# Weighing one condition vector of the second layer's modulation on GpSimd instead of TensorE

## The reference, cut to what matters

```
c_act = jax.nn.silu(c)
for layer in range(DEPTH):
    mod = c_act @ w_ada[layer] + b_ada[layer]
    sh1, sc1, g1, sh2, sc2, g2 = jnp.split(mod[:, None, :], 6, axis=-1)
    h = rmsnorm(x, mix_norm_g[layer]) * (1.0 + sc1) + sh1
    y = ...                      # layer 1: differential attention with 8 heads
    x = x + g1 * y
    h = rmsnorm(x, ffn_norm_g[layer]) * (1.0 + sc2) + sh2
    x = x + g2 * hierarchical_moe(h, ...)
```

```
bias = jnp.where(allowed[None], -slopes[:, None, None] * dist[None], -jnp.inf)
s1 = einsum(qa, k1) * scale + bias;   s2 = einsum(qb, k2) * scale + bias
p = softmax(s1) - lam * softmax(s2);  o = p @ v
```

## Time and profile before

| what | value |
|---|---|
| median of 3 runs | 1230.32 us (1229.67 to 1231.67) |
| the profiled execution: its own time | 1232.17 us |
| the profiled execution: its span | 1230.3 us |
| PE busy | 893.5 us (73%) |
| DVE busy | 350.8 us (29%) |
| ACT busy | 169.9 us (14%) |
| POOL busy | 23.6 us (2%), 70 instructions |
| DMA | 490.05 MB, mean 398 GB/s |
| chain that ended last | DMA 50%, PE 41%, SP's queue 3%, DVE 3% |

### The profile page before, as it was taken

The page is one execution under the profiler, slowest core; times in us unless marked ns, Lnnn a source line. Parts: engine busy times, 40 slices in busy tenths (PEclk is TensorE's granted clock), DMA queues, the critical chain, the costliest instruction groups (busy, mean ns, idle before and its releaser), DMA issues.

```text
span 1230.3 us, 14582 instructions
## 1 busy us (share of the span) xinstructions
PE 893.5 (73%) x6026; PEld 436.7 (35%) x6026; DVE 350.8 (29%) x893; ACT 169.9 (14%) x408; POOL 23.6 (2%) x70
## 2 busy tenths in 40 slices
PE   6999997747474756656799999966475665665647
PEld 5867453222131312121278554632131212121212
DVE  2298544121111111111124647521111111202111
ACT  1124340000000000000133353300000000000000
POOL 1001100000000000000000100000000000000000
PEclk9999999788787878787899999988787878777888
DMA  9999999999999999999995959699999999999996
GB/s 344 395 400 409 412 398 421 428 428 426 428 428 429 427 429 428 430 426 428 400 408 212 346 218 362 256 425 425 428 429 427 427 429 429 428 429 427 428 425 263
DMA packets 63224, 490.05 MB, mean 398 GB/s; under 512 B 5664, under 2 KB 8113, under 8 KB 39616
## 3 DMA queue, kind: packets, MB, share of 16 engines
q1 hardware_dynamic: 60656, 486.56, 95.4%
q10 hardware_dynamic: 2512, 2.69, 0.6%
HBM read 488.18 MB, written 1.05 MB: 398 GB/s over the span
## 4 chain that ended last, share of the span: by engine, by line
DMA 50%; PE 41%; SPq 3%; DVE 3%; issue 1%; ACT 1%; POOL 0%; DVEq 0%; ACTq 0%
PE psum L1649 41%; DMA weight_ring<-in_moe_w_down 18%; DMA weight_ring<-in_moe_w_gate 17%; DMA weight_ring<-in_moe_w_up 14%; SPq L499 2%; DMA weight_ring<-in_w_ada 1%; SPq L522 1%; DVE h_or_mix_T L1126 0%; PE psum L1748 0%; DVE ada_partials L1567 0%; ACT phase_region L907 0%; ACT phase_region L1027 0%; DVE phase_region L1601 0%; DVE phase_region L1213 0%; DVE phase_region L1096 0%
## 5 line engine op out<-in xcount | busy, mean ns | idle before, releaser
L1649 PE MATMUL psum<-weight_ring,h_or_mix_T 128*32 128x512 f32 (+1 forms) x2240 | 384.3, 711 | 232.3 <-DMA weight_ring<-in_moe_w_gate 140.8
L1649 PEld LDWEIGHTS psum<-weight_ring,h_or_mix_T 128*32 128x32 f32 (+1 forms) x2240 | 119.0, 136 | 479.1 <-issue 477.2
L1649 PE MATMUL psum<-weight_ring,ada_partials 128*32 128x512 f32 (+1 forms) x1088 | 141.2, 675 | 77.7 <-DMA weight_ring<-in_moe_w_down 72.8
L1649 PE MATMUL psum<-phase_region 128*128 128x128 f32 (+5 forms) x824 | 154.8, 349 | 4.1 <-DVE x_tokens L1377 1.3
L1649 PEld LDWEIGHTS psum<-phase_region 128*128 128x128 f32 (+2 forms) x824 | 99.4, 188 | 75.7 <-issue 54.8
L1649 PE MATMUL psum<-h_or_mix_T,weight_ring 128*128 128x256 f32 (+1 forms) x528 | 115.0, 374 | 2.8 <-DVE h_or_mix_T L1126 2.7
L1649 PEld LDWEIGHTS psum<-h_or_mix_T,weight_ring 128*128 128x128 f32 x528 | 97.3, 190 | 17.4 <-DVE h_or_mix_T L1126 1.9
L1649 PEld LDWEIGHTS psum<-weight_ring,ada_partials 128*32 128x32 f32 x1088 | 41.0, 126 | 168.2 <-issue 158.7
L1426 DVE SCALAR_TENSOR_TENSOR phase_region<-phase_region,psum 128x512 f32<-128x512 f32 x16 | 11.0, 688 | 235.6 <-ACT phase_region L940 235.6
L1442 DVE TENSOR_TENSOR phase_region<-psum,gate_rows 128x512 f32<-128x512 f32 x28 | 19.4, 692 | 205.5 <-PE psum L1649 205.5
L1431 DVE SCALAR_TENSOR_TENSOR ada_partials<-phase_region,psum 128x512 f32<-128x512 f32 x16 | 16.8, 1051 | 211.9 <-PE psum L1649 211.9
(11 more groups left out here) (222 smaller groups left out, 486.7 us busy)
## 6 DMA issues: line engine op xcount, KB each, us to landing
weight_ring<-in_moe_w_up SPq DMA_DIRECT2D x64, 2048.0 KB, 20.2
weight_ring<-in_moe_w_gate SPq DMA_DIRECT2D x62, 2048.0 KB, 20.3
weight_ring<-in_moe_w_down SPq DMA_DIRECT2D x60, 2048.0 KB, 19.7
weight_ring<-in_w_ada SPq DMA_DIRECT2D x10, 3072.0 KB, 21.3
weight_ring<-in_odd_w_in SPq DMA_DIRECT2D x6, 2048.0 KB, 22.9
weight_ring<-in_w_ada SPq DMA_DIRECT2D x10, 1024.0 KB, 23.2
weight_ring<-in_w_ada SPq DMA_DIRECT2D x4, 2048.0 KB, 17.7
weight_ring<-in_even_w_in SPq DMA_DIRECT2D x3, 2048.0 KB, 21.0
```

Source lines behind the costliest of these rows:

```text
L1649: return pe.matmul(out_, lhsT, rhs, start=first, stop=last, **kw)
```

## The change

Row 10 is no longer summed by 32 matmuls. GpSimd multiplies each of the eight rows of the slab, in its slot, by the condition's column and adds rows 1 to 7 onto row 0: 8 multiplications and 7 additions of 128x1024, each linked to the next by a semaphore. They are written in pairs of rows in front of the bias tiles of heads 2 to 5. TensorE then sums the one row that is left over the partitions with 4 matmuls, in head 4 (`add_pool_rows`) and not in head 3. `take_modulation(10)` moves from head 3 to head 4 on DVE, and the copy `CREP1` goes.

```diff
-        CREP1 = NEGS[:, :, :].rearrange("p a (k n) -> p (a k) n", n=32)
...
+        pool_weighted = sem("pool_weighted")
...
+            def weigh(n, lo, hi):
+
+                s = slab_index("ada", n)
+                rows = wide(s)
+                for k in range(lo, hi):
+                    if k == 0:
+                        pool.wait_ge(slab_in[SPOT[s]], landed(s, 0))
+                    if k == ADA_FIRST:
+                        pool.wait_ge(rest_in[SPOT[s]], landed(s, 1))
+                    link(g.tensor_scalar(rows[:, k, :], rows[:, k, :], CCOL[:, 1, k:k + 1], None, ALU.mult))
+                    if k:
+                        ins = g.tensor_tensor(rows[:, 0, :], rows[:, 0, :], rows[:, k, :], ALU.add)
+                        if k == KD - 1:
+                            ins.then_inc(pool_weighted, 1)
+                        else:
+                            link(ins)
...
             for h in range(NH):
+                if 2 <= h < 6:
+                    weigh(10, 2 * (h - 2), 2 * (h - 1))
                 if h == 0:
                     pool.wait_ge(qk_out, 16)
...
-            v.tensor_copy(CREP1[:, :, :], CCOL[:, 1, :].unsqueeze(2).broadcast_to([P, KD, 32])).then_inc(cond_in_place, 1)
...
-                if h == 3:
+                if h == 4:
                     take_modulation(10)
...
+            def add_pool_rows():
+
+                pe.wait_ge(ada_ready, 10)
+                pe.wait_ge(v_out, 4)
+                pe.wait_ge(pool_weighted, 1)
+                rows = wide(slab_index("ada", 10))[:, 0, :]
+                for g in range(4):
+                    ins = mm(PS[32 * g:32 * g + 32, ADA_BANK[10], 0:256], ONES[:, 0:32], rows[:, 256 * g:256 * g + 256],
+                             True, True, skip_group_check=True)
+                ins.then_inc(ada_summed, 1)
...
-                if h == 3:
-                    pe.wait_ge(v_out, 4)
-                    modulation_sums(10)
+                if h == 4:
+                    add_pool_rows()
```

More of the change, by code:

```diff
@@ L335, in build_trunk @@
         PART_SLOT = {6: 2, 7: 3, 5: 1}
-        ADA_HEAD = ADA_ORDER[:8]
         def sums_by(n):
@@ L1668, in modulation_sums @@
                     slab_ready(s)
-                    if n == 10:
-                        pe.wait_ge(cond_in_place, 2)
                     if n in (3, 5):
@@ L1673, in modulation_sums @@
                     elif n > 1:
-                        pe.wait_ge(ada_ready, {2: 1, 6: 2, 7: 3, 4: 4, 10: 10}[n])
-                cond = CREP if n in ADA_HEAD else CREP1
+                        pe.wait_ge(ada_ready, {2: 1, 6: 2, 7: 3, 4: 4}[n])
                 for k in range(lo, hi):
@@ L1679, in modulation_sums @@
                     for g in range(4):
-                        ins = mm(PS[32 * g:32 * g + 32, ADA_BANK[n], 0:256], cond[:, k, :], wide(s)[:, k, 256 * g:256 * g + 256],
+                        ins = mm(PS[32 * g:32 * g + 32, ADA_BANK[n], 0:256], CREP[:, k, :], wide(s)[:, k, 256 * g:256 * g + 256],
                                  k == 0, k == KD - 1, skip_group_check=True)
```

## The result

The changed kernel takes 1244.42 us (median of 4 runs, 1242.6 to 1245.23) against 1229.99 us before in the same comparison: ratio 1.0113, 95% interval 1.0101 to 1.0125, so 14.4 us slower. I had forecast 1235.4 us and a range up to 1240.0. The direction was right, the size not.

The account below looks back on a forecast made before the run. TensorE's work in the heads (700 to 757 us) was taken to move the kernel's end one for one; -3.6 + 1.4 - 0.2 + 7.5 = +5.1 us on the median 1230.3 gave 1235.4 us, range 1227.8 to 1240.0.

Parts of the forecast that it names:

- Head 3, head 4, the copy: 32 matmuls leave head 3, -3.6 us; four matmuls and `take_modulation(10)` enter head 4, +1.4; `CREP1` goes, -0.2.
- the price of the multiplication: On GpSimd, one multiplication of 1024 takes 1.04 us, drawn from fills and a bias tile; eight of them in the work.
- DVE's waits: In heads 0 to 2 DVE waits for GpSimd's instructions under way: +7.5 us, bounds 0 and 11.8.
- So no bias tile is late: GpSimd's work ends about 725 us, before `biased(5)` wants its bias tile at 727.55: no late tile.
- rival C: GpSimd itself too slow: at 3.0 us an addition, head 5's bias tile is 5.3 us late, 1233.2 us; chance 0.08.
- my own signs of being wrong: Wrong if DVE's lines keep their durations, bias tiles come late, or the last mixture starts late for want of weights.
- My upper bound: For DVE's waits: 4.4 us for each of three heads less twice 0.7, 11.8 us, if an addition takes 2.6.
- The clock is not in play: In the heads, 700 to 757 us, TensorE's clock is granted at 1.00, the 2.4 GHz level; no term for it.
- Lock or sharing: DVE and GpSimd lock each other out for a whole instruction, as the sum assumes, or share bandwidth, near the fourth case.
- rival D: DVE waits once a head for 0.8 us, no GpSimd instruction gets between its own: -1.4, 1228.9 us; chance 0.17.
- The slot: Slot 2 is free some 11 us later, in head 4; weights behind it still in time: counted 0, up to 6 us.

Follow-up runs that it names:

- none: The changed kernel with GpSimd's 15 operations on the slab left out, so row 10 is a bare row of weights: 1227.55 us.
- imm: The changed kernel with the condition's column in GpSimd's multiplications replaced by two constants, 0.5 and 0.0: 1240.61 us.
- actbias: The changed kernel, all of it computed, with the bias tiles of heads 2 to 7 made by ACT and not by GpSimd: 1237.51 us.
- prodonly: The changed kernel without GpSimd's eight multiplications and with its seven additions turned into products of two slab rows: 1238.64 us.
- multonly: The changed kernel with GpSimd's seven additions left out and its eight multiplications by the column kept: 1230.04 us.
- memset: The changed kernel with GpSimd's multiplications and additions replaced by fills of nearly the same total time: 1244.88 us.
- dve: The kernel before, with row 10 weighed by DVE in its idle time behind heads 0 to 4 and four matmuls in head 4: 1227.64 us.

## Why the prediction was right or wrong

**Head 3, head 4, the copy: right.** -3.6, +1.4 and -0.2 were forecast, -2.4 in sum; **none** measured -2.3, with both heads' periods to 0.01 us. The copy shows in the traces by itself: from the same DVE step ahead of the norm (611.99 us before, 611.85 now) to TensorE's first matmul behind it (622.63, 622.29) it is 10.64 us before and 10.44 now.

Two steps failed: the price of the multiplication and the size of DVE's waits. GpSimd's work cost 16.9 us and not 7.5; of the 9.4 us between them 3.8 go with the first and 5.6 with the second, which has a lower clock of TensorE in it.

**The price of a multiplication: wrong, and the step that failed first.** "a multiplication of 1024 is 0.51 + 640 x 0.83 = 1.04 us" took its slope from fills and its base from a bias tile, which multiplies by a constant. With a constant it is right to 0.01 us (**imm**: 1.047). The change's multiplication takes its factor from a column in SBUF, and that form had no row in the trace: 3.0 us. I gave bounds for the addition, which also had no row, and none for this. Eight times 2 us are 16 us more of GpSimd's work. From **imm** to the changed kernel it is 3.8 us of time.

**"So no bias tile is late": wrong, by that step.** With 11.6 us a head the tiles of heads 3, 4 and 5 came late and GpSimd became the pace; against **actbias** this cost 6.9 us. It is rival C, whose mechanism I priced by a dear addition and not by the multiplication, and for which I left 0.08. Late bias tiles were also one of my own signs of being wrong.

**DVE's waits: right in kind, too small, and the larger of the two misses.** The forecast was 7.5 us. At the multiplication's price that I had assumed the loss is 13.1 us (**imm**), from seven additions alone 11.1 (**prodonly**), and in the change with the tiles in time about 10 (**actbias**). So even had the multiplication cost what I assumed, the sum would have been 5.6 us short, and 1240.61 us lie just past the end of the range. The rule that each engine is held up for the length of the other's instruction held beside the additions and the multiplications by a constant. It did not hold beside the change's own multiplications by the column, which take 3.0 us and cost no step of DVE more than 1.0 (**multonly**). Wrong besides was my guess of how often. A waiting GpSimd instruction was to get in "once for certain and, I guess, once more in every other head"; in **imm** the difference for head 0 met it at lines 1639, 1644 and 1648, and its chain grew by 5.3 us, not 3.5: 2.09 + 0.80 + 2.36, the first and the last behind an addition each. The dearer addition (2.35, not 1.9) adds to every one of them. My upper bound had a slip too: by the prediction's own formula an addition of 2.6 us gives 4.6 us a head and 12.3 in all, not 4.4 and 11.8. The estimate of 2.2 us by the Trainium skill's "GPSIMD Engine Reference", section "3.1 Elementwise — side-by-side cycle accounting", was the better one: an addition measures 2.35.

**"The clock is not in play": wrong.** I read it from a row of the kernel before, where TensorE hardly waits, and put the term at nothing. In **imm** 3.5 of the 13.1 us are TensorE's own work at a lower granted clock, in **prodonly** 2.6 of 11.1, and in the changed kernel 1.6 us in head 5. Without this part DVE's waits in **imm** are 9.3 us.

**Lock or sharing: the lock.** The Trainium skill, "SBUF — State Buffer", section "Who interferes with whom", says that a DVE instruction with two SBUF inputs contends only with a GpSimd instruction that reads SBUF, and its fast single-input ones with either. **memset** agrees: beside fills the multiply-adds keep 0.75 us while the scaling of two numbers takes 0.92. The multiplications by the column don't fit a lock held for the whole instruction (**multonly**), and there the measurement decides. Sharing (rival D, 0.17) can't turn 0.23 us into 2.32. These waits have no semaphore, so my sentence ahead of the forecast that the engines meet at semaphores alone was wrong as well: DVE and GpSimd meet here too.

**The slot: right in cost.** SP issued the next tenants of slot 2 at 749.48 us, 18 us later than before (731.15) and not 11, as the heads were later, and the last mixture's first piece is unchanged at 16.44 us.

**The range** ended at 1240.0 because its upper bound was built from DVE's waits alone, with the late tiles in another case. The rival with the low chance was the one that joined the forecast's own mechanism; joined ends belong in the range.

## What to carry to other kernels

An operation's price is taken from a row of the same form, operand kinds included; where a form has no row, it gets bounds, above all when only a small part of it (constant or column) is new. Work on an "idle" GpSimd is not hidden if DVE, on a chain with 0.7 us to spare, has short instructions from SBUF to SBUF: each can pay for a whole GpSimd instruction in front of it, so seven of 2.35 us cost 11, part of it by TensorE's lower clock behind the waits. A clock read at 1.00 holds for the kernel that was traced, not for one with new waits. Look first for idle time on the engine that already does such work: the same rows went into DVE's gaps for nothing that could be measured (**dve** 1227.64 us, **none** 1227.55).

## What the runs showed of the hardware that I had not expected

GpSimd, 128x1024 in place, f32: multiplication by a constant 1.047 us, by a column as scalar operand 2.84 to 3.1 (the first, beside DVE's multiply-add, 3.68), by the same column repeated as a tensor 1.89, sum or product of two full rows 2.35, fill 0.95. The slowest form troubles DVE least: beside the 3.0 us multiplications of **multonly** no step of DVE's difference lost more than 1.0 us (the two multiply-adds, 1.73 instead of 0.75), and the transposes of head 4 came 1.7 us later than in **none**. It doesn't let everything through: in the same run the scaling of two numbers passed in its 0.23 us at 710.13, in the middle of a multiplication, and the two scalings behind it, started at 710.27, took 1.38 us instead of 0.54 and ended at 711.65, just after the multiplication (711.50). Why was not tried.

TensorE's clock fell. In 753 to 761 us of the changed kernel, and in the same stretch before, where later work stands (us, busy of the engines, clock, DMA share, GB/s):

```profile
753.00:761.00 8.00, 7.30 (x23) 3.83 (x24) 6.00 (x21) 3.19 (x11) 0.00 (x0) 0.79 1.02 432
```

```profile
753.00:761.00 8.00, 8.00 (x23) 4.04 (x23) 5.92 (x6) 1.76 (x5) 0.00 (x0) 1.00 0.85 294
```

The granted clock is 0.79, so part of the stretch ran at the 1.2 GHz level, and TensorE had waited 10.7 us for DVE in five of the heads, the last time just before 753.70. Head 5 took 7.60 us where **none** needs 5.95 for the same work: 1.6 us of the loss come from the clock, not from any wait. Head 0 was slow in the same way (7.20 us for 5.52, clock 0.76), but there GpSimd's pace covered it.

The waits alone don't say when it falls. **multonly** has the same 7.60 us for head 5, at a clock of 0.78, with waits for DVE's difference of 4.1 us in all. **imm** and **memset**, with waits for DVE of 11.0 and 11.5 us, have 5.96 us for it at 1.00. In all of these and in **none** TensorE waited 1.71 or 1.72 us just before head 5. In **imm** the clock fell in heads 0 and 1 instead, right behind the waits of 5.77 and 3.55 us. What sets it was not tried apart.
